# Moving three modulation sums of a one-core decoder block to turns 62, 65 and 68

## The reference, cut to what matters

```
mod = (silu(c) @ w_mod + b_mod)          # 6 x 2048: sh1, sc1, g1, sh2, sc2, g2
h = rms_norm(x, norm1_g) * (1 + sc1) + sh1
z = h @ w_in                             # FoX q,k,v,forget | NSA q,k,v,gates | conv a,g
mix = concat(fox_attention(z), nsa_attention(z), conformer_conv(z))
x = x + g1 * (mix @ w_out)
h = rms_norm(x, norm2_g) * (1 + sc2) + sh2
x = x + g2 * (relu(h @ w_mlp1)**2 @ w_mlp2)
out = rms_norm(x, final_g)
```

## Time and profile before

| | |
|---|---|
| three executions | 1186.18 to 1186.96 us, median 1186.9 |
| the profiled execution | 1185.15 us, its span 1183.1 us |
| PE (matmul) busy | 1139.2 us, 96% of the span |
| DVE busy | 989.9 us, 84% |
| ACT busy | 638.0 us, 54% |
| chain that ended last | PE 75%, DVE 11%, DMA 6%, ACT 4%, issue 4% |
| mean granted TensorE clock | 0.986 |

### The profile page before, as it was taken

How to read it: one execution, slowest core, us unless ns; L and a number is a source line. 1 busy time by engine, 2 the same in 40 slices (tenths; PEclk the granted TensorE clock), 3 DMA queues, 4 the chain that set the end, 5 groups by cost and what they waited for, 6 DMA issues and landing times.

```text
span 1183.1 us, 17839 instructions
## 1 busy us (share of the span) xinstructions
PE 1139.2 (96%) x7081; PEld 1007.9 (85%) x7081; DVE 989.9 (84%) x1197; ACT 638.0 (54%) x929; POOL 23.5 (2%) x40
## 2 busy tenths in 40 slices
PE   4998999999999998999999999999999999999996
PEld 4898989998877777999788888888888888888885
DVE  5998989989889988996887787987788987778675
ACT  6655448877664546445544445544445554445452
POOL 2000000100000000001000000000000000000000
PEclk7999999999999999999999999999999999999998
DMA  9999998878957897995657676566675657766451
GB/s 375 421 420 420 420 379 308 264 197 297 310 207 256 290 309 268 380 384 181 209 186 266 236 276 208 183 213 249 250 265 196 208 188 273 257 217 260 162 178 71
DMA packets 48322, 314.65 MB, mean 266 GB/s; under 512 B 6572, under 2 KB 8440, under 8 KB 11768
## 3 DMA queue, kind: packets, MB, share of 16 engines
q1 hardware_dynamic: 44592, 305.72, 69.9%
q0 software_dynamic: 1760, 5.26, 2.3%
q10 hardware_dynamic: 1896, 2.64, 0.8%
HBM read 305.20 MB, written 4.21 MB: 262 GB/s over the span
## 4 chain that ended last, share of the span: by engine, by line
PE 75%; DVE 11%; DMA 6%; ACT 4%; issue 4%; SPq 0%; ACTq 0%; DVEq 0%
PE quad L1249 15%; PE quad L1263 10%; PE quad L1265 10%; PE quad L1264 10%; PE quad L1251 8%; PE quad L1239 5%; PE quad L1241 5%; PE quad L1240 5%; DMA mod_raw<-in_w_mod 3%; DMA first_raw<-in_w_mod 2%; DVE w_lo L1796 2%; DVE mod_raw L1803 2%; PE quad L1310 2%; PE quad L1311 2%; PE quad L1309 2%
## 5 line engine op out<-in xcount | busy, mean ns | idle before, releaser
L870 ACT ACTIVATE w_hi<-raw 128x1024 fp32r<-128x1024 f32 (+1 forms) x342 | 355.4, 1044 | 312.2 <-PE quad L1265 119.9
L1796 DVE TENSOR_TENSOR w_lo<-raw,w_hi 128x1024 fp32r<-128x1024 f32 (+1 forms) x342 | 408.6, 1205 | 116.3 <-ACT w_hi L870 114.5
L1249 PE MATMUL quad<-act,w_hi 128*128 128x512 f32 x768 | 266.4, 390 | 0.0
L1239 PE MATMUL quad<-act,w_hi 128*128 128x256 f32 x760 | 215.8, 284 | 7.3 <-DVE w_lo L1796 5.2
L1251 PE MATMUL quad<-act,w_lo 128*128 128x256 f32 x768 | 216.6, 282 | 0.0
L1240 PE MATMUL quad<-act,w_hi 128*128 128x256 f32 x760 | 213.7, 281 | 0.0
L1241 PE MATMUL quad<-act,w_lo 128*128 128x256 f32 x760 | 213.5, 281 | 0.0
L1249 PEld LDWEIGHTS quad<-act,w_hi 128*128 128x128 f32 x768 | 144.2, 188 | 30.1
L1239 PEld LDWEIGHTS quad<-act,w_hi 128*128 128x128 f32 x760 | 144.5, 190 | 10.0 <-issue 7.2
L1263 PE MATMUL quad<-w_hi,u_hi 128*128 128x512 f32 x376 | 148.9, 396 | 0.6 <-DVE u_lo L2266 0.6
L1265 PE MATMUL quad<-w_hi,u_lo 128*128 128x512 f32 x376 | 148.8, 396 | 0.0
(11 more groups left out here) (367 smaller groups left out, 1712.5 us busy)
## 6 DMA issues: line engine op xcount, KB each, us to landing
raw<-in_w_main SPq DMA_DIRECT2D x184, 1024.0 KB, 5.1
mod_raw<-in_w_mod SPq DMA_DIRECT2D x72, 1024.0 KB, 7.1
first_raw<-in_w_mod SPq DMA_DIRECT2D x14, 1024.0 KB, 14.7
late_raw<-in_w_mod SPq DMA_DIRECT2D x10, 1024.0 KB, 8.2
conv_b<-conv_q POOLq DMA_DIRECT2D x8, 512.0 KB, 5.9
x_a<-in_x SPq DMA_DIRECT2D x2, 1024.0 KB, 7.1
x_scratch<-x SPq DMA_DIRECT2D x1, 2048.0 KB, 12.8
x<-x_scratch SPq DMA_DIRECT2D x1, 2048.0 KB, 10.6
```

The source lines that it names most:

```text
L870: A(dst[:, 0:2 * width], block_half(raw, j, width), ACT.Copy).then_inc(hi_done, 1)
L1239: mm(out, hi, act_hi[:, k, :], start=begin and m % 2 == 0, stop=False, skip_group_check=True)
L1249: mm(out, w_hi[j % 4][:, cols], act_both[:, k, :, :].rearrange("p h t -> p (h t)"), start=begin, stop=False, skip_group_check=True)
L1796: TTn(lo[:, 0:2 * width], block_half(raw, j, width), hi[:, 0:2 * width].bitcast(f32), ALU.subtract)\
```

## The change

It alters the plan `MODS_AT` alone. Turns 62, 65 and 68 get one sum each; turns 81, 95 and 96 lose theirs. As the sums run in the order of m, every sum from 39 to 47 moves: 39, 40 and 41 go from turns 76, 78 and 80 to turns 62, 65 and 68; 42 to 47 go from turns 81, 82, 84, 86, 95 and 96 to turns 76, 78, 80, 82, 84 and 86. From sum 48 on nothing moves. The number of sums, their operands and their buffers stay.

```diff
 MODS_AT = {turn: 1 + (turn in (9, 21, 27, 33)) for turn in range(5, 60, 2) if turn != 45}
-MODS_AT |= {FOX_AT + AHEAD + t: 1 for t in (1, 3, 5, 6, 7, 9, 11)}
-MODS_AT |= {NSA_TURN + t: 1 for t in (0, 1, 4, 7, 9, 13, 14, 15, 17, 18, 19, 20, 21, 23)}
+MODS_AT |= {turn: 1 for turn in (62, 65, 68)}
+MODS_AT |= {FOX_AT + AHEAD + t: 1 for t in (1, 3, 5, 7, 9, 11)}
+MODS_AT |= {NSA_TURN + t: 1 for t in (4, 7, 9, 13, 14, 15, 17, 18, 19, 20, 21, 23)}
 MODS_AT |= {NSA_TURN + t: 2 for t in (5, 11)}
```

## The result

The changed kernel takes 1189.2 us (median of 12 executions, 1187.3 to 1192.4), the kernel before, on the same chips, 1186.9 (12 executions, 1184.3 to 1188.5). The ratio is 1.0023, with a 95% interval from 1.0014 to 1.0033: slower, by 2.7 us by the ratio and 2.3 by the medians, little but clear of no change. The prediction was 1188.2, between 1184.9 and 1190.6.

The account below looks back on a forecast made before the run. PE, busy 96% of the span, was taken as the bound, so only its waits count. Terms +3.2 - 1.9 + 0 + 0 = +1.3 us gave 1186.45 profiled, 1188.2 as expected median; range 1184.9 to 1190.6.

Parts of the forecast that it names:

- rival (a): Tap DMAs become the bound at ACT's product of tap 17, from mean landing over 7.8 us; 1190.5 at 8.6; chance 0.15.
- The lead and the loss on PE: Turns 62 to 68: 6.62 us of sums come in, DVE's lead covers 3.73, PE loses 2.89 before halves 68 and 69.
- rival (b): DVE's lead before half 69 is larger than read, so only the gain is left: 1185.0 us; chance 0.10.
- What queues behind: ACT's products and splits after tap 15, then DVE's scores of turn 75: 3.2 us in all, between 2.9 and 3.4.
- Turn 81: Sum removed ahead of the `w_lo` of half 82: scores and transposes come earlier, PE gains 1.9 us, bounds 0 and 2.2.
- rival (c): The gain does not come: turn 83 scores are held by something else, the loss stands alone; 1190.1 us; chance 0.07.
- Turns 95 and 96: Sums removed at the second attention's start: DVE gets 4.5 us, PE is full and gets nothing; costed at 0.
- rival (e): The sums of turns 95 and 96 were in the way after all: 1183.7 us; chance 0.05.
- rival (d): The clock falls at the two new PE stalls, costing 1.7 us: 1189.9 us; chance 0.06.
- The loads: Moved loads and later weight quarters, three 1 MB loads added to 203 to 236: taken as 0, upper bound 2.3 us.
- L: Landing time of a tap DMA, taken as 6.3 us; its delay shows from 7.8 us on.
- The formula: ACT reaches tap 17's product by the DMAs at 209.1 + 3L + 4, against about 236.6 by its own chain.

Follow-up runs that it names:

- one sum, turn 62: Against the changed kernel: only one sum moved, to turn 62; turn 81 has none, turns 95 and 96 keep theirs; 1186.2 us, ratio 1.0002.
- two sums: Against the changed kernel: sums in turns 62 and 65 only; turns 81 and 96 have none, turn 95 keeps its; 1188.4 us, ratio 1.0017.
- short loads: Changed kernel with the loads of blocks 41 to 43 cut to their first 64 of 2048 columns; 1188.4 us, ratio 1.0021.
- before, sums 46 and 47 short: Kernel before, with sums 46 and 47 (turns 95 and 96) cut to 64 columns; 1186.7 us, ratio 1.0007.
- short tap DMAs: Changed kernel with all nine tap DMAs cut to 32 partitions of one channel tile, 32 KB instead of 512; 1187.5 us, ratio 1.0007.
- one sum, short tap DMAs: Against the changed kernel: one sum at turn 62, none at turn 81, and tap DMAs cut to 32 KB; 1184.6 us, ratio 0.9985.
- one sum, turn 64: Against the changed kernel: one sum at turn 64 in place of 62, none at turn 81, nothing left out; 1186.3 us, ratio 0.9995.
- two out of crowded turns: Against the changed kernel: sums at turns 64 and 91, none at turn 81, one instead of two at turn 100; 1181.6 us, ratio 0.9956.
- the turn-64 kernels: Two kernels with a sum at turn 64 and the same plan up to turn 90, one also with a sum at turn 91; 1186.3 and 1181.6 us.

## Why the prediction was right, and which term was too small

Set side by side, with what the account of the traces says and what was timed (each ratio less 1, times 1186.9), in us:

| kernel | scores of turn 75 late | turn 81 | turn 100 | sum | timed |
|---|---|---|---|---|---|
| the change | 4.81 | -1.9 | 0 | +2.9 | +2.7 |
| one sum, turn 62 | 2.17 | -1.9 | 0 | +0.3 | +0.2 |
| two sums | 4.23 | -1.9 | 0 | +2.3 | +2.0 |
| short loads | 4.54 | -1.9 | 0 | +2.6 | +2.5 |
| before, sums 46 and 47 short | 0.00 | 0 | 0 | 0 | +0.8 |
| short tap DMAs | 3.18 | -1.9 | 0 | +1.3 | +0.8 |
| one sum, short tap DMAs | 0.08 | -1.9 | 0 | -1.8 | -1.8 |
| one sum, turn 64 | 1.28 | -1.9 | 0 | -0.6 | -0.6 |
| two out of crowded turns | 0.01 | -1.9 | -2.7 | -4.6 | -5.2 |

The side and the range held, and most terms did. But the time alone doesn't tell the forecast from rival (a): 1189.2 lies between 1188.2 and 1190.5. The traces do. By the prediction's own sign, a wait of ACT for the tap DMA before tap 17 (0.52 us, and 4.64 and 2.06 before that), rival (a) came, to which the prediction had given 0.15. That the range held is due to its width, which took in both. Term by term:

- **The lead and the loss on PE.** 6.54 us came in for 6.62, and PE reached half 69 2.82 us later for 2.89. The bracketed waits show 0.73 + 1.61 = 2.3 of it; starts are the safer measure. With one sum no `w_lo` wait came, with two 0.7: the lead of 3.73 was read rightly, and rival (b) falls.
- **What queues behind.** 3.2, and 3.18 once the tap DMAs are out of the way.
- **Turn 81.** 1.9, and 1.90 in the trace; rival (c) falls.
- **Turns 95 and 96.** 0: from turn 83 to 99 nothing moved, and cutting these sums gained nothing; rival (e) falls.
- **The clock.** It stayed at its full level beside both new stalls, where the busy view (PE, PEld, DVE, ACT, POOL, clock, DMA share, GB/s) has

```profile
222.00:226.00 4.00, 3.27 (x29) 3.10 (x28) 3.89 (x6) 4.00 (x9) 0.59 (x1) 1.00 1.02 376
226.00:230.00 4.00, 2.47 (x22) 2.27 (x20) 3.97 (x4) 1.95 (x5) 0.00 (x0) 1.00 0.79 179
```

  with 1.5 us of standing still in four and a clock of 1.00, the 2.4 GHz level; rival (d) did not come at this place.
- **The loads: the term that was too small.** The prediction said "I take 0, and 2.3 at L = 8.6 as the upper bound". It measured 1.6. The formula was good: with the measured landings in place of 3L and the issue at 208.76, 208.8 + 10.9 + 7.7 + 6.2 + 4 = 237.6, and ACT's product of tap 17 starts at 237.86. What was wrong was L = 6.3, taken because most tap DMAs of before took about that. The three measured ones have a mean of 8.3, above the 7.8 from which it shows. So rival (a) came in at two thirds of its price: 1188.2 + 1.6 = 1189.8, beside 1189.2. The 1.6 is a difference of two profiled executions, and the turn-64 kernels show that such a reading can differ by 1.3; the difference of the ratios, 1.9, bears it out.
- **Why L was misjudged.** I counted the loads' bytes against the free share of the DMA engines, and let "the later DVE spreads the quarters" speak against (a). The short loads show the opposite: with hardly any of those bytes the landings are 8.9, 9.6 and 6.1, a mean of 8.2 against 8.3, because a sum shifts the next quarter to the tap DMA's issue. The step lacked a line for each quarter: its issue before, plus the sums ahead of it, beside each tap's issue.

The Trainium skill, DMA: Bandwidth & Descriptors, "Issuing engines are not separate DMA queues", has all engines' transfers interleave on the same 16 DMA engines. The landings agree with it: 6.2 us for tap 8 before, 10.9 beside a load and a quarter.

What stays open: whether another order of SP's issues (the quarter after the tap DMA) would keep three sums cheap; it was not tried. Most of the 1.2 us behind turn 99 in the profile after goes with a stretch at a lower granted clock, which follows a stall of PE that left the clock at 1.00 before; why it fell in one execution and not in the other isn't shown.

## What to carry to other kernels

Before work is put into a "free" stretch of an engine, write down the lead in us of that engine over the bound one and don't put in more than that; here one sum fitted and three didn't. Then list what else that engine's later progress releases: for one sum, a weight transfer shifted next to a new load cost more than the work itself, and the same plan gained 1.8 us with a tap DMA of 32 KB behind the two, and nothing with one of 512 KB. And look for the turns in which the moved work stands right ahead of the bound engine's input, with a wait of its own (turn 100), not for those in which the engine looks busy (turns 95 and 96, worth nothing).

## What the runs showed of the hardware that was not expected

The landing time of a small DMA was set by what was issued beside it more than by its own size. The 32 KB tap DMA landed after 2.1 us when alone. The DMA view of the change with short tap DMAs, at the issue for tap 8 (209.0 to 209.5):

```profile
raw<-in_w_main SPq DMA_DIRECT2D x1, 1024.0 KB, 7.9
conv_b<-conv_q POOLq DMA_DIRECT2D x1, 32.0 KB, 7.6
```

and at the issue for tap 14 (226.4 to 226.9):

```profile
conv_b<-conv_q POOLq DMA_DIRECT2D x1, 32.0 KB, 2.1
```

In the first, a load was issued 1.2 us and a quarter 0.03 us ahead of it, 2 MB in all. A megabyte takes about 2.5 us of the DMA engines (an estimate from the 426 GB/s of the earlier trace rows), so 5.5 us more is about the time of these two: the small one lands with the last of them (0.2 us ahead of it), not in proportion to its share. Sixteen times the bytes beside the same two transfers took 10.9 us, 3.3 more. Behind a single quarter, issued 0.55 us ahead and landing after 5.1 us, the 32 KB take 4.8, as the DMA view of the one-sum kernel with short tap DMAs has it for tap 14:

```profile
conv_b<-conv_q POOLq DMA_DIRECT2D x1, 32.0 KB, 4.8
```

and 4.9 and 5.0 for two more. The Trainium skill, DMA: Bandwidth & Descriptors, "Queues, rings and completion order", says that a semaphore increment lands only after every earlier write from its DMA engine, across queues. By that rule a small DMA is told as done only when what its engines wrote before it is written, and the 4.8 behind the 5.1 agrees: it landed 0.2 us after the quarter. But the order of the data itself adds to it. Among the packets of that trace, the first of the 32 KB starts 3.6 us after the issue, against 1.3 when alone (tap 14 above), and 123 of the quarter's 128 have started by then, so these two did not take turns packet by packet. Beside the load and the quarter they overlap more (74 other packets start between the first and the last of the 32 KB), so a strict order isn't shown.
